# Stick-breaking sums in two float32r halves, with the softplus split across ScalarE, VectorE and GpSimd

## The reference

```python
def sb_block(q, qpos, k, v, kpos, sb_bias):
    z = (jnp.einsum('bqhd,bkhd->bhqk', q, k).astype(jnp.float32) * HEAD_DIM ** -0.5
         + sb_bias.astype(jnp.float32)[None, :, None, None])
    causal = (kpos[None, :] < qpos[:, None])[None, None]
    log_1mb = jnp.where(causal, jax.nn.log_sigmoid(-z), 0.0)
    suffix = lax.cumsum(log_1mb, axis=3, reverse=True) - log_1mb
    a = jnp.where(causal, jnp.exp(jax.nn.log_sigmoid(z) + suffix), 0.0)
    return jnp.einsum('bhqk,bkhd->bqhd', a.astype(v.dtype), v)
```

## Time and profile before

| | |
|---|---|
| median of 3 runs | 2492.29 us (2487.1 to 2492.31) |
| profiled execution | 2494.33 us, its span 2492.5 us |
| TensorE busy | 2253.5 us, 90% of the span |
| VectorE busy | 904.7 us, 36% |
| ScalarE busy | 648.8 us, 26% |
| GpSimd busy | 103.6 us, 4% |
| mean granted TensorE clock | 0.954 of 2.4 GHz |

### The profile page before, as it was taken

The page is one execution under the profiler, slowest core; times in us unless marked ns, Lnnn a source line. Parts: engine busy times, 40 slices in busy tenths (PEclk is TensorE's granted clock), DMA queues, the critical chain, the costliest instruction groups (busy, mean ns, idle before and its releaser), DMA issues.

```text
span 2492.5 us, 32587 instructions
## 1 busy us (share of the span) xinstructions
PE 2253.5 (90%) x13604; PEld 1829.6 (73%) x13604; DVE 904.7 (36%) x1270; ACT 648.8 (26%) x1016; POOL 103.6 (4%) x188
## 2 busy tenths in 40 slices
PE   7999999999676588898899999679999999999998
PEld 6999999999445444444445577348889888988896
DVE  6120021111116425454444422362443344334435
ACT  5211111111221245455541113252111111111113
POOL 3110010001200000000000000000000000000000
PEclk9999999999877779999999999799999999999999
DMA  6867752111750435455453322201111111111101
GB/s 213 275 232 260 246 198 62 53 54 39 281 209 1 182 113 156 144 158 172 140 153 134 131 71 85 68 1 43 34 51 51 34 36 50 51 34 47 41 32 72
DMA packets 146132, 274.61 MB, mean 110 GB/s; under 512 B 10921, under 2 KB 83394, under 8 KB 145218
## 3 DMA queue, kind: packets, MB, share of 16 engines
q1 hardware_dynamic: 129874, 181.50, 22.8%
q10 hardware_dynamic: 2656, 46.80, 5.5%
q0 software_dynamic: 13456, 44.23, 4.9%
HBM read 244.72 MB, written 73.77 MB: 128 GB/s over the span
## 4 chain that ended last, share of the span: by engine, by line
PE 78%; DVE 9%; ACT 7%; issue 3%; DMA 3%; PEldq 0%; SPq 0%; PEld 0%; ACTq 0%; DVEq 0%; POOL 0%
PE psum L1628 13%; PE psum L1002 12%; PE psum L1006 12%; PE psum L1004 12%; PE psum L983 5%; PE psum L1457 2%; PE psum L1414 2%; PE psum L1520 1%; PE psum L1272 1%; PE psum L1306 1%; PE psum L1308 1%; PE psum L1307 1%; PE psum L1479 1%; PE psum L1427 1%; PE psum L1379 1%
## 5 line engine op out<-in xcount | busy, mean ns | idle before, releaser
L1002 PE MATMUL psum<-h0H,w0H 128*128 128x368 f32 (+1 forms) x1080 | 239.0, 330 | 0.6 <-DVE w0L L2191 0.6
L1006 PE MATMUL psum<-h0H,w0L 128*128 128x368 f32 (+1 forms) x1080 | 237.2, 328 | 0.0
L1004 PE MATMUL psum<-h0L,w0H 128*128 128x368 f32 (+1 forms) x1080 | 237.0, 328 | 0.0
L2552 DVE TENSOR_TENSOR xt<-psum,xt 128x1024 f32<-128x1024 f32 x144 | 174.6, 1221 | 138.5 <-PE psum L1628 138.5
L1628 PE MATMUL psum<-wH,hidH 128*128 128x512 f32 (+1 forms) x576 | 179.6, 393 | 11.4 <-DVE xt L2552 11.4
L1006 PEld LDWEIGHTS psum<-h0H,w0L 128*128 128x128 f32 x1080 | 185.6, 188 | 0.0
L1004 PEld LDWEIGHTS psum<-h0L,w0H 128*128 128x128 f32 x1080 | 185.6, 188 | 0.0
L1002 PEld LDWEIGHTS psum<-h0H,w0H 128*128 128x128 f32 x1080 | 184.5, 188 | 0.9 <-DVE w0L L2191 0.9
L1628 PE MATMUL psum<-wH,hidL 128*128 128x512 f32 (+1 forms) x576 | 177.7, 390 | 0.0
L1628 PE MATMUL psum<-wL,hidH 128*128 128x512 f32 (+1 forms) x576 | 177.5, 389 | 0.0
L1004 PE MATMUL psum<-hTL,wH 128*128 128x368 f32 x744 | 163.3, 328 | 0.0
(11 more groups left out here) (309 smaller groups left out, 3140.3 us busy)
## 6 DMA issues: line engine op xcount, KB each, us to landing
RA<-in_cache_sb_k SPq DMA_DIRECT2D x128, 256.0 KB, 2.9
RA<-in_cache_sb_v SPq DMA_DIRECT2D x128, 256.0 KB, 2.9
RA<-in_w_in SPq DMA_DIRECT2D x46, 512.0 KB, 5.7
PA<-in_w_up SPq DMA_DIRECT2D x16, 1024.0 KB, 5.1
PA<-in_w_down SPq DMA_DIRECT2D x16, 1024.0 KB, 4.9
out<-in_cache_win_k ACTq DMA_DIRECT2D x8, 2040.0 KB, 9.1
out<-in_cache_win_v ACTq DMA_DIRECT2D x8, 2040.0 KB, 14.8
RA<-in_cache_win_k SPq DMA_DIRECT2D x26, 512.0 KB, 7.7
```

What stands on the lines that cost most here:

```text
L1002: pe.matmul(out, wh, rhs_high[:, k, a:b], start=(k == 0), stop=False)
L1004: pe.matmul(out, wh, rhs_low[:, k, a:b], start=False, stop=False)
L1006: last = pe.matmul(out, wl, rhs_high[:, k, a:b], start=False, stop=(k == len(high) - 1))
L2552: nc.vector.tensor_tensor(xt[0:n, t, :], psum[0:n, at:at + 1024], xt[0:n, t, :], ALU.add).then_inc(s_ev, 1)
```

## The change

In the stick-breaking stage:

- `spb` has one buffer instead of two. The triangle and the ones are kept as `negtriR` and `negonesR` in float32r, and TensorE waits for them once.
- `pair_high` (new, ScalarE) rounds the softplus into `spH`; `pair_low` (new, VectorE) writes the rest into `spL`. Both have one buffer. `pair_exponent` adds the products of both halves.
- `running_split` (new, GpSimd) makes the halves `RpH` and `RpL` of the running sum, in two buffers; `sample_split` and `sample_running_split` (new, GpSimd) do the same for the sample's softplus and running sums. `sample_exponent` takes the halves.
- `pair_log` works on one head at a time, four instructions instead of two, and the semaphores of clamp, log, softplus and halves count heads.
- The sample exponent moves from the second to the third step, `sample_weigh` behind the page copies of that step, `sample_running` from the second step to the third, behind the low half. The page values move from the third step to the first of the next group, the page scores behind the exponent. The value pages are loaded 12 behind the key pages instead of 8.
- GpSimd loads the first gate tile before the stage and the second one only behind it.

Outside the stage several transfers now share semaphores (`s_mem`, `s_pg`), with a wait of SP in front of some, and four waits of an engine on itself go through `link`.

```diff
-                nc.scalar.activation(z, z, ACT.Ln, bias=1.0).then_inc(s_bl, 1)
+                for e in range(2):
+                    act.wait_ge(s_bz, 2 * t + e + 1)
+                    last = nc.scalar.activation(zb[:, e, lo:512], zb[:, e, lo:512], ACT.Exp)
+                link(last)
+                for e in range(2):
+                    nc.scalar.activation(zb[:, e, lo:512], zb[:, e, lo:512], ACT.Ln, bias=1.0).then_inc(s_bl, 1)
+
+            def pair_high(t):
+                lo = lo_of(t)
+                if t:
+                    act.wait_ge(s_bc, t)
+                for e in range(2):
+                    act.wait_ge(s_bsp, 2 * t + e + 1)
+                    nc.scalar.copy(spH[:, e, lo:512], spb[:, e, lo:512]).then_inc(s_bh, 1)
...
+            def pair_low(t):
+                lo = lo_of(t)
+                if t:
+                    dve.wait_ge(s_bc, t)
+                for e in range(2):
+                    dve.wait_ge(s_bh, 2 * t + e + 1)
+                    nc.vector.tensor_tensor(spL[:, e, lo:512], spb[:, e, lo:512], spH[:, e, lo:512].bitcast(F32), ALU.subtract
+                                            ).then_inc(s_bw, 1)
...
+            def running_split(t):
+                k, lo, n = place(t), lo_of(t), sum_no[t]
+                b = (k + 1) % 2
+                gp.wait_ge(s_bR, n + 1)
+                if t >= 1:
+                    gp.wait_ge(s_bc, t)
+                nc.gpsimd.tensor_copy(RpH[:, b, :, lo:512], Rp[:, b, :, lo:512]).then_inc(s_bRw, 1)
+                gp.wait_ge(s_bRw, 2 * n + 1)
+                nc.gpsimd.tensor_tensor(RpL[:, b, :, lo:512], Rp[:, b, :, lo:512], RpH[:, b, :, lo:512].bitcast(F32),
+                                        ALU.subtract).then_inc(s_bRw, 1)
...
             def pair_exponent(t):
                 lo = lo_of(t)
-                pe.wait_ge(s_bsp, t + 1)
                 for e in range(2):
-                    last = pe.matmul(zbank(t, e)[:, lo:512], negtri[:, :], spb[:, t % 2, e, lo:512], start=False,
-                                     stop=first_of(t), skip_group_check=True)
+                    pe.wait_ge(s_bh, 2 * t + e + 1)
+                    pe.matmul(zbank(t, e)[:, lo:512], negtriR[:, :], spH[:, e, lo:512], start=False, stop=False,
+                              skip_group_check=True)
+                    pe.wait_ge(s_bw, 2 * t + e + 1)
+                    last = pe.matmul(zbank(t, e)[:, lo:512], negtriR[:, :], spL[:, e, lo:512], start=False, stop=first_of(t),
+                                     skip_group_check=True)
```

## The result

| | before | after |
|---|---|---|
| median | 2492.3 us (2485.5 to 2494.2, 6 runs) | 2505.4 us (2501.7 to 2506.5, 6 runs) |
| ratio, with its 95% interval | | 1.0061 [1.0047, 1.0075] |
| span of the profiled execution | 2492.5 us | 2503.9 us |
| first pair scores to first branch product | 866.5 to 1330.4, 463.9 us | 860.1 to 1338.6, 478.5 us |
| of it the second and third head pair | 109.5 and 108.3 us | 112.5 and 112.6 us |

The stick-breaking stage is 14.6 us longer. It begins 6.4 us earlier and the part behind it is 3.2 us longer, which together makes the 11.4 us of the spans.

The account below looks back on a forecast made before the run. TensorE was taken to bound the stage before, a ScalarE-VectorE loop after; loop and lateness 366 + lock 43 + clock 7 = 416 us, 16 less than 432, giving 2476 us, range 2428 to 2512.

Parts of the forecast that it names:

- TensorE's 62 us: Stick-breaking stage: float32r halves of the negtri, negones and sample products take 62 us off TensorE's 383 us busy.
- 344 us the stage: Stage length if TensorE stayed the bound: 432 - 62 - 26 = 344 us.
- The sample exponent's 26 us: Moving the sample exponent to the third step removes TensorE's waits of 20.3 and 5.8 us there.
- Loop and lateness, 91.5 us per head pair: Loop through ScalarE and VectorE, high copy to high copy: 81.6 us per head pair, plus 9.9 lateness; stage 366 us.
- lateness: TensorE's next scores come after the clamp could start, and a page copy delays ScalarE's log: 9.9 us per head pair.
- The lock, 43 us (20 to 75): GpSimd's splits and VectorE's operations with two SBUF inputs lock each other out: 43 us in the stage, bounds 20 and 75.
- the first rival: Lock is cheap: low halves follow on each other, GpSimd waits; stage 366 to 395, time 2426 to 2455 us; chance 0.22.
- The clock, 7 us: TensorE waits for page copies and its granted clock suffers in the stage: 7 us added, between -8 and 30.
- a sign of being wrong: The prediction is wrong if TensorE's granted clock in the stage falls below 0.9.
- Nothing outside the stage: Shared or renamed semaphores outside the stage cost nothing; without cover, one landing, 3 to 7 us.
- The sum: Stage 366 + 43 + 7 = 416 us, 16 less than 432; time 2476 us.
- The slower rival: Lock serialises cast, subtraction and both low halves in nearly every step with a running sum; stage 459, time 2519; chance 0.26.

Follow-up runs that it names:

- b2: Kernel before, each float32 negtri and negones product replaced by two float32r products reading a tile filled once, sample exponent unmoved; 2478.6 us, ratio 0.9967.
- b1: Kernel before with only the sample exponent moved to the third step, ahead of the pair's; 2476.0 us, ratio 0.9952.
- a1: Changed kernel without GpSimd's splits from the second head pair on, later running sums and sample halves left out; 2467.1 us, ratio 0.9918 to before.
- e2: d2 with the sample's logarithm behind the late page copy, its softplus and sums behind the third step's clamp; 2446.6 us, ratio 0.9839 to before.
- d2: c1 with the sample exponent's two products in float32 and without the two sample splits; 2477.2 us, ratio 0.9956 to before.
- d4: Kernel before plus 80 GpSimd instructions splitting the running sums' widths on a constant tile, results unread; 2489.1 us, ratio 0.9999.
- a2: Changed kernel with GpSimd's split of the running sum waiting for both low halves of the step; 2507.7 us, ratio 1.0079 to before.
- c1: Changed kernel with the sample's running sums on VectorE behind the pair's clamp instead of ahead of it; 2464.7 us, ratio 0.9915 to before.
- e1: c1 without GpSimd's splits from the second head pair on, later running sums and sample halves left out; 2442.1 us, ratio 0.9823 to before.
- e3: c1 with the sample's work moved behind the pair's as in e2, sample halves still split on GpSimd; 2463.7 us, ratio 0.9898 to before.
- f2: e2 with GpSimd's split of the pair sums waiting for both low halves, as in a2; 2439.1 us, ratio 0.9793 to before.

## Where the prediction failed

- **TensorE's 62 us.** The prices were right: the products start 0.22 to 0.24 us apart, and the four of a sample take 0.9 us for 1.7. What was wrong was to call 344 us the stage "if TensorE stayed the bound": alone the saving is worth 9.4 us (b2), for the next waits stood right behind it. This did not enter the sum, which went by the loop, but it gave the forecast its sign by a wide cushion that is not there.
- **The sample exponent's 26 us.** The wait went, as forecast. In b1 only 13.4 us of it reach the end; page-turn waits grew from 10.6 to 20.5 us in two head pairs. This term did not enter the sum either.
- **Loop and lateness, 91.5 us per head pair: the step that failed.** With the clock's term it was 93.2; a1 shows 99.5 without a lock, 25 us more for the stage. The prediction counted from one high copy of ScalarE to the next; measured so, in us for the four steps of each kind in a head pair (a1: second and third head pair):

| steps | forecast, without lock | a1 | after |
|---|---|---|---|
| first | 22.9 | 29.2, 32.0 | 33.5 |
| second | 29.2 + 9.9 lateness | 39.1, 39.1 | 39.1 |
| third | 29.5 | 30.4, 30.5 | 40.1 |

  The second steps came out as forecast, and the lateness too: their clamps wait 9.6 us per head pair for scores. What failed is the overlap assumed in first steps, where no lateness was counted. There the clamp also waits for the scores, in a1 0.85 to 1.80 us in each first step of the second head pair, 5.0 together, and 7.5 in the third. On TensorE these scores stand behind the late page turn, which waits for ScalarE, and behind the four products of the sample exponent, which the change moved in front of them; of a1:

```profile
1067.50 0.63 PE L1511 MATMUL psum<-ident,RA 128*128 128x128 f32 x4 [1.34 <-ACT RQ L1882]
1067.88 0.48 PE L1553 MATMUL psum<-spSH,negtriR 128*128 128x512 f32 x1
1068.67 0.40 PE L1557 MATMUL psum<-RSL,negonesR 128*128 128x512 f32 x1
1069.00 1.13 PE L1463 MATMUL psum<-RQ 64*128 64x512 f32 x4
1070.17 1.41 DVE L2365 TENSOR_SCALAR RA<-psum,sbb 128x512 f32<-128x512 f32 x2 [0.90 <-PE psum L1463]
```

  That the exponent's place is the reason is read from this order; no run moved it elsewhere with all else kept. The 30.6 us of e2 against d2 are another matter: they come mostly out of the second steps (39.1 to 34.3 us per head pair), whose length the prediction had right.
- **The lock, 43 us (20 to 75): right in kind, 51 us by a1.** Its place was wrong. I put 1.7 us into a first step of full width and 2.3 into a third one. Second steps lose nothing, as forecast; the four third steps of a cycle lose 9.6 us together, and the first ones 1.5 to 4.3 (the table). By the distances of the pair scores three of the four third steps lose 2.7 to 5.3 us each (the fourth has no running sum) and the others nearly nothing. Low halves are lengthened in steps of every kind, but in first and second steps the clamp behind them waits for its scores anyway. Here and there the two low halves follow each other without a gap and GpSimd is the one that waits, as the first rival had it. One such second step of after, then a first step with the lock (2.14 us for 1.29) and the clamp's wait behind it:

```profile
1062.00 1.29 DVE L2387 TENSOR_TENSOR spL<-RA,spH 128x512 fp32r<-128x512 f32 x2
1062.15 2.04 POOL L966 CAST RpH<-RA 128x1024 fp32r<-128x1024 f32 x1 [6.72 <-DVE RA L2409]
1083.40 2.14 DVE L2387 TENSOR_TENSOR spL<-RA,spH 128x512 fp32r<-128x512 f32 x2
1086.84 1.41 DVE L2365 TENSOR_SCALAR RA<-psum,sbb 128x512 f32<-128x512 f32 x2 [1.30 <-PE psum L1463]
```

  In third steps the sample's split is already running when the first low half could start. There I had priced the five sample operations once (1.5 us) and not seen that each of them is locked in turn while the clamp, ScalarE and TensorE stand behind. GpSimd's subtraction of 1024 columns takes 2.36 us undisturbed (d4); the 1.9 taken was low. (The memset of rows 7 is 0.93 ns a column, not 0.83; the sum used its 0.95 us.) The price from the Trainium skill, "GPSIMD Engine Reference", in the section on performance versus the Vector engine, which made about 2.3 us, was the better one; the trace agrees with it.
- **The clock, 7 us.** It fell to 0.88, below the 0.9 that the prediction named as a sign of being wrong. TensorE's busy time per head pair is 85.6 us with the splits and 82.1 without, so the splits' waits cost at most 3.5 us per head pair more through the clock; how much of that lies on the path no run tells. In a1 the clock is 0.93 already, so the 7 us can't be told from the chain's term, and the 25 us above are what is left when they are taken as right.
- **Nothing outside the stage:** no run contradicts it, within the 7 us by which what lies behind it varies.
- **The sum.** 416 + 25 (chain) + 8 (lock) = 449 us, against 4 x 112.6 = 450 measured; the two corrections are read from a1, so this is bookkeeping and no test. The stage of before was also read short: it begins at 866.5 us, not 897, and its four head pairs are 436 us, not 432. The range held the time; the forecast of faster fell mainly by the chain term, in which first steps had no lateness. The slower rival had its sign right but only half of its mechanism: the lock lengthens low halves in most steps, but costs time almost only in the third ones.

## What to carry to other kernels

Before giving an engine less work, read which wait comes next behind it: with TensorE 90% busy in before, 62 us less of its work were worth 9. Where engines run by written orders, ask of every small job that is moved what stands behind it on its engine; five sums of 1.5 us together ahead of a clamp cost 15 to 19 us by themselves and 41 with a second engine's lock on top, and a job pushed back on ScalarE alone cost 17. And put an instruction of GpSimd that reads SBUF where VectorE has only operations with a PSUM operand: there 80 of them cost nothing.

## What the runs showed of the hardware

- The lock also catches VectorE's copies, which have a single SBUF operand: 128 columns take 0.22 us alone, and 0.86 on average in after. The Trainium skill, "SBUF — State Buffer", section "Who interferes with whom", says so of copies that can run in a two-port mode; the prediction had counted only operations with two SBUF operands. The clamp and the softplus, with one operand in PSUM, keep their 0.75 us in after, a1, a2, c1, e1, e2 and e3.
- GpSimd pays as well: its cast of 1024 columns takes 1.04 us undisturbed and 1.58 in after, the subtraction 2.36 and 2.56.
- Behind many waits of 2.0 to 5.2 us TensorE ran at 1.2 GHz for a while (pair scores 2.08 us for 1.13, a page turn 1.08 for 0.60), and such a wait cost up to 1 us more than itself. It did not behind every one: in e1 a page turn behind a wait of 3.19 us took 0.63 us and the scores behind it 1.13; in f2 it ran at 1.2 GHz behind one wait of 2.01 us and at 2.4 GHz behind one of 1.76.
